# A PEER layer on one core: 8 more tokens by gathered expert rows, 376 dense columns, gate products on GpSimd

## The reference, cut to what matters

```python
def peer(a, w_q, k1, k2, u_exp, v_exp):        # a: (1, 512, 2048)
    ...                                         # two key scores of 128, their best 16 x 16 pairs, the best 16 of these
    experts = jnp.take_along_axis(cand_idx, sel, axis=-1)      # (1, 512, 8, 16), numbers below 16384
    gates = jax.nn.softmax(top, axis=-1)
    def one(args):
        a_c, e_c, g_c = args
        u_sel = jnp.take(u_exp, e_c, axis=0)
        h = jnp.einsum('bthkd,btd->bthk', u_sel, a_c, preferred_element_type=jnp.float32)
        w = (g_c * jax.nn.gelu(h)).astype(a_c.dtype)
        v_sel = jnp.take(v_exp, e_c, axis=0)
        return jnp.einsum('bthk,bthkd->btd', w, v_sel)
```

## Time and profile before

| | us |
|---|---|
| median of 3 runs | 3154.93 (3150.54 to 3158.9) |
| the profiled execution | 3154.94 |
| its span, first to last instruction | 3152.8 |
| TensorE busy | 3112.9 |
| VectorE busy | 2191.3 |
| GpSimd busy | 1066.6 |
| ScalarE busy | 1064.2 |

### The profile page before, as it was taken

The page is one execution under the profiler, slowest core; times in us unless marked ns, Lnnn a source line. Parts: engine busy times, 40 slices in busy tenths (PEclk is TensorE's granted clock), DMA queues, the critical chain, the costliest instruction groups (busy, mean ns, idle before and its releaser), DMA issues.

```text
span 3152.8 us, 42300 instructions
## 1 busy us (share of the span) xinstructions
PE 3112.9 (99%) x16812; PEld 2925.5 (93%) x16812; DVE 2191.3 (70%) x3012; ACT 1064.2 (34%) x1291; POOL 1066.6 (34%) x559
## 2 busy tenths in 40 slices
PE   8999999999999999999999999999999999999998
PEld 6888668899999999999999999999999999999887
DVE  5465653478787777777777647888878887776545
ACT  5234442332333333333333333333333333334422
POOL 1010000028888878788888201101111111110000
PEclk9999999999999999999999999999999999999999
DMA  8472212235455699999999767888888887884322
GB/s 303 144 257 91 94 54 104 96 121 133 115 130 122 176 350 349 322 342 335 352 338 347 276 247 291 309 317 313 302 311 308 315 320 292 319 313 175 107 93 94
DMA packets 190974, 739.10 MB, mean 234 GB/s; under 512 B 69904, under 2 KB 123152, under 8 KB 130944
## 3 DMA queue, kind: packets, MB, share of 16 engines
q1 hardware_dynamic: 90768, 409.55, 35.8%
q0 software_dynamic: 81648, 302.68, 28.3%
q10 hardware_dynamic: 18432, 25.17, 2.3%
HBM read 682.60 MB, written 54.72 MB: 234 GB/s over the span
## 4 chain that ended last, share of the span: by engine, by line
PE 86%; POOL 8%; issue 2%; DVE 2%; DMA 2%; ACT 0%; SPq 0%; DVEq 0%; ACTq 0%; POOLq 0%
PE ps L1492 28%; PE ps L1493 28%; PE ps L1494 28%; POOL gates L460 7%; POOL rows L474 2%; DMA gates<-gates_r,idx_d 1%; PE ps L1665 1%; PE ps L1684 1%; PE ps L1664 0%; DMA raw<-s_v 0%; PE ps L1727 0%; DVE wL L845 0%; DVE ssum L857 0%; DMA rows<-uv_rows,idx_s 0%; PE ps L1674 0%
## 5 line engine op out<-in xcount | busy, mean ns | idle before, releaser
L1492 PE MATMUL ps<-aH,wH 128*128 128x384 f32 (+2 forms) x3088 | 1087.0, 352 | 6.2 <-DVE wL L845 4.0
L1493 PE MATMUL ps<-aL,wH 128*128 128x384 f32 (+2 forms) x3088 | 1083.4, 351 | 0.0
L1494 PE MATMUL ps<-aH,wL 128*128 128x384 f32 (+2 forms) x3088 | 1083.3, 351 | 0.0
L492 ACT ACTIVATE wH<-raw 128x2048 fp32r<-128x2048 f32 x333 | 637.9, 1916 | 893.6 <-PE ps L1494 715.9
L460 POOL DMA_INDIRECT gates<-gates_r,idx_d x384 | 793.2, 2066 | 384.5 <-DVE gates_r L1237 238.3
L845 DVE TENSOR_TENSOR wL<-raw,wH 128x2048 fp32r<-128x2048 f32 x333 | 762.2, 2289 | 230.0 <-ACT wH L492 223.4
L1492 PE MATMUL ps<-actH,wH 128*128 128x384 f32 x2048 | 684.1, 334 | 0.0
L1494 PE MATMUL ps<-actH,wL 128*128 128x384 f32 x2048 | 684.0, 334 | 0.0
L1493 PE MATMUL ps<-actL,wH 128*128 128x384 f32 x2048 | 684.0, 334 | 0.0
L1492 PEld LDWEIGHTS ps<-aH,wH 128*128 128x128 f32 x3088 | 580.7, 188 | 46.7 <-DVE wL L845 5.5
L1494 PEld LDWEIGHTS ps<-aH,wL 128*128 128x128 f32 x3088 | 580.7, 188 | 38.4
(11 more groups left out here) (240 smaller groups left out, 1808.4 us busy)
## 6 DMA issues: line engine op xcount, KB each, us to landing
raw<-s_pu SPq DMA_DIRECT2D x128, 1024.0 KB
raw<-s_pv SPq DMA_DIRECT2D x128, 1024.0 KB
gates<-zeros POOLq DMA_DIRECT2D x24, 1024.0 KB, 8.7
pre<-ut ACTq DMA_DIRECT2D x128, 192.0 KB
pre_in<-pre SPq DMA_DIRECT2D x128, 192.0 KB, 4.4
gate_in<-gates SPq DMA_DIRECT2D x128, 192.0 KB
raw<-s_out SPq DMA_DIRECT2D x16, 1024.0 KB
raw<-s_pq SPq DMA_DIRECT2D x16, 1024.0 KB
```

The costliest lines, as they stand in the source:

```text
L492: A(wH[parity][:, :], raw[parity][:, :], ACT.Copy).then_inc(hi_ready, 1)
L1492: mm(out, wh, xh, start=start, stop=False)
L1493: mm(out, wh, xl, start=False, stop=False)
L1494: return mm(out, wl, xh, start=False, stop=stop)
```

## The change

The dense part shrinks to 376 tokens (`TD`, `TA` = 384 is where the gathered 128 begin), so the matmuls of stages u and v, the stored activations, the gate table and the elementwise passes on them have 376 columns instead of 384. Tokens 376 to 383 are computed by gathered rows in a different layout: 128 partitions hold 16 sets of these 8 tokens, one set for each head and half of its 16 picks, so that 8 more gathers (`B_PICKS`) cover all their 1,024 picks. 32 small transfers bring their expert numbers and gates to these partitions; the 8 token columns are normed, repeated 16 times and transposed to banks 0 to 3 (`spread_tokens`); at the end 16 matmuls with `sel`, in which each token's column picks its 16 partitions, sum the sets. The tiles of v move to banks 4 to 7. The products of activations and gates move from VectorE to GpSimd. 60 picks instead of 64 are worked at up to slot 117, 4 more (`LATE`) in slots 120 to 127, and 72 instead of 64 in stage v.

```diff
 TOPK = 16
 KEYS = 128
 EPS = 1e-6
-TD = 384
-NTD = TD // P
-PICKS = HEADS * TOPK
+BT = 8
+TA = T - P
+TD = TA - BT
+NTD = NT - 1
+SETS = P // BT
+PARTS = SETS // HEADS
+A_PICKS = HEADS * TOPK
+B_PICKS = TOPK // PARTS
+PICKS = A_PICKS + B_PICKS
 GROUP = 8
 NGROUPS = KEYS // GROUP
-BACK = [0, 1, 6, 7]
+BACK = [0, 1, 2, 3]
 WIDE = 2048 // GROUP
 HEAD_U = 4
 ROUTE_U = HEAD_U * HEADS
 ADDS_FIRST = 176
 FIRST_PICK, LAST_PICK = ROUTE_U + 4, KEYS - GROUP - 2
-U_PICKS = 64
+U_PICKS, LATE = 64, 4
 FIRST_SLOT = 2
+B_PREP = 1
 
 
 def u_step(c):
 
-    return (min(max(c, FIRST_PICK), LAST_PICK) - FIRST_PICK) * 2 * U_PICKS // (LAST_PICK - FIRST_PICK)
+    if c > KEYS - GROUP:
+        return 2 * (U_PICKS - LATE + min((c - KEYS + GROUP + 1) // 2, LATE))
+    return (min(max(c, FIRST_PICK), LAST_PICK) - FIRST_PICK) * 2 * (U_PICKS - LATE) // (LAST_PICK - FIRST_PICK)
 
...
@@ -61,7 +70,7 @@
 
 ROW_AT, ROW_USED, ROW_TURN = [], [], []
 for _j in range(PICKS):
-    _at = _j % 3 if _j < U_PICKS else 3 + _j % 2
+    _at = _j % 3 if _j < U_PICKS - LATE else 2 if _j < U_PICKS else 3 + _j % 2
     ROW_USED.append(max([j for j in range(_j) if ROW_AT[j] == _at], default=-1))
     ROW_TURN.append(1 + ROW_AT.count(_at))
     ROW_AT.append(_at)
...
     a_tok = at("a_tok", [KD, T], F, A0 + 32 * KB)
+    b_rep = a_tok[:, :, 0:P]
+    b_small = a_tok[:, :, P:P + BT]
...
             nu = S0["pu"] - ROUTE_U
-            with sp.Fori(0, (KEYS - GROUP - ROUTE_U) // 2) as i:
+            for c in range(ROUTE_U, ROUTE_U + 8):
+                load(nu + c, stream["pu"][c, :, :], c % 2)
+            sp.wait_ge(routed, HEADS)
+            at_b = TD - (NTD - 1) * P
+            for h in range(HEADS):
+                for r in range(PARTS):
+                    dst = slice((h * PARTS + r) * BT, (h * PARTS + r + 1) * BT)
+                    src = slice(h * TOPK + r * B_PICKS, h * TOPK + (r + 1) * B_PICKS)
+                    sp.dma_start(idx_b[dst, :], idx_e[at_b:P, src]).then_inc(b_loaded, 16)
+                    sp.dma_start(gates_b[dst, :], gates_r[at_b:P, NTD - 1, src]).then_inc(b_loaded, 16)
+            with sp.Fori(4, (KEYS - GROUP - ROUTE_U) // 2) as i:
                 for b in range(2):
                     load(nu + ROUTE_U + 2 * i + b, stream["pu"][ROUTE_U + 2 * i + b, :, :], b)
 
...
@@ -368,6 +398,7 @@
                 if c == KEYS - GROUP:
                     for b in range(2):
                         sp.wait_ge(gates_added[b], 16 * NTD * TOPK * HEADS // 2)
+                    sp.wait_ge(b_loaded, 32 * SETS)
                 load_chunk(c - KEYS + GROUP, c % 2)
 
             def load_values(g, last=False):
...
+                    out=gates_flat, out_offset=bass.IndirectOffsetOnAxis(ap=idx_d[0:m, t, c:c + 1], axis=0),
+                    in_=gates_r[0:m, t, c:c + 1], in_offset=None, compute_op=ALU.add).then_inc(gates_added[h % 2], 16)
 
             added = ADDS_FIRST
             for n in range(added):
                 add_gates(n)
 
             pool.wait_ge(a_tok_ready, 1)
-            for j in range(PICKS):
+
+            def gather(j):
+
                 if j == U_PICKS:
                     pool.wait_ge(tile_done, CUM[S0["pv"] - 1])
+                if j == A_PICKS:
+                    pool.wait_ge(b_loaded, 32 * SETS)
                 if ROW_USED[j] >= 0:
                     pool.wait_ge(pick_done, ROW_USED[j] + 1)
+                ids = idx_s[:, j:j + 1] if j < A_PICKS else idx_b[:, j - A_PICKS:j - A_PICKS + 1]
                 pool.indirect_dma_start(
                     out=rows[ROW_AT[j]][:, :, :].rearrange("p a d -> p (a d)"), out_offset=None, in_=a["uv_rows"],
-                    in_offset=bass.IndirectOffsetOnAxis(ap=idx_s[:, j:j + 1], axis=0)).then_inc(row_landed[ROW_AT[j]], 16)
-                if j >= 2:
+                    in_offset=bass.IndirectOffsetOnAxis(ap=ids, axis=0)).then_inc(row_landed[ROW_AT[j]], 16)
+
+            def apply_gates(c, b):
+
+                pool.wait_ge(pre_loaded[b], (c - b) * 8 + 16)
+                pool.wait_ge(gates_loaded[b], (c - b) * 8 + 16)
+                nc.gpsimd.tensor_tensor(pre_in[b][:, :], pre_in[b][:, :], gate_in[b][:, :], ALU.mult).then_inc(act_gated, 1)
+
+            for j in range(U_PICKS - LATE + 1):
+                gather(j)
+                if j >= 1:
                     for n in range(added, min(added + 4 - j % 2, HEADS * NTD * TOPK)):
                         add_gates(n)
                         added = n + 1
+            assert added == HEADS * NTD * TOPK
+            for c in range(GROUP):
+                apply_gates(c, c % 2)
+                if c % 2 == 0 and U_PICKS - LATE + 1 + c // 2 < U_PICKS:
+                    gather(U_PICKS - LATE + 1 + c // 2)
+            for j in range(U_PICKS, U_PICKS + 2):
+                gather(j)
+            for g in range(NGROUPS - 1):
+                for q in range(GROUP):
+                    apply_gates(GROUP * (g + 1) + q, q % 2)
+                    for o in range(v_step(g, q), v_step(g, q + 1)):
+                        if o % 2 == 1 and o // 2 + 2 < PICKS:
+                            gather(o // 2 + 2)
 
 
         @block.scalar
...
+                for o in range(u_step(c), u_step(c + 1)):
+                    if o % 2 == 0:
+                        weigh_pick(o // 2)
                 weight_hi(c - KEYS + GROUP, c - KEYS + GROUP, 0, pre_in[c % 2])
             nv = S0["pv"]
 
...
+            V.scalar_tensor_tensor(a_tok[:, :, TA:T], hT[:, :, TA:T], rtok[:, NTD:NTD + 1],
                                    gain_row[:, :].rearrange("p (a b) -> p a b", a=KD), ALU.mult, ALU.mult).then_inc(a_tok_ready, 1)
             dve.wait_ge(a_tok_ready, 1)
 
             def dot(j):
 
                 dve.wait_ge(row_landed[ROW_AT[j]], 16 * ROW_TURN[j])
+                if j == A_PICKS:
+                    dve.wait_ge(b_tok_done, 1)
+                if j < A_PICKS:
+                    act_of, d = a_tok[:, :, TA:T], dots[:, j:j + 1]
+                else:
+                    act_of = ps[:, 0:4, :].rearrange("p b (c d) -> p (b c) d", c=4)
+                    d = dots_b[:, j - A_PICKS:j - A_PICKS + 1]
                 r3 = rows[ROW_AT[j]][:, 0, :].rearrange("p (a b) -> p a b", a=KD)
-                V.scalar_tensor_tensor(r3, r3, 1.0, a_tok[:, :, TD:T], ALU.mult, ALU.mult,
-                                       accum_out=dots[:, j:j + 1]).then_inc(dot_done, 1)
+                V.scalar_tensor_tensor(r3, r3, 1.0, act_of, ALU.mult, ALU.mult, accum_out=d).then_inc(dot_done, 1)
 
             def add_row(j):
 
                 dve.wait_ge(pick_weighed, j + 1)
                 if j >= 1:
                     dve.wait_ge(pick_done, j)
-                V.scalar_tensor_tensor(hT[:, :, TD:T], rows[ROW_AT[j]][:, 1, :].rearrange("p (a b) -> p a b", a=KD),
-                                       pick_w[:, j:j + 1], hT[:, :, TD:T], ALU.mult, ALU.add).then_inc(pick_done, 1)
+                v3 = rows[ROW_AT[j]][:, 1, :].rearrange("p (a b) -> p a b", a=KD)
+                if j < A_PICKS:
+                    V.scalar_tensor_tensor(hT[:, :, TA:T], v3, pick_w[:, j:j + 1], hT[:, :, TA:T],
+                                           ALU.mult, ALU.add).then_inc(pick_done, 1)
+                elif j == A_PICKS:
+                    V.tensor_scalar(b_acc, v3, pick_wb[:, 0:1], None, ALU.mult).then_inc(pick_done, 1)
+                else:
+                    V.scalar_tensor_tensor(b_acc, v3, pick_wb[:, j - A_PICKS:j - A_PICKS + 1], b_acc,
+                                           ALU.mult, ALU.add).then_inc(pick_done, 1)
+
+            def spread_tokens():
+
+                st.did(V.tensor_tensor(b_small, hT[:, :, TD:TA],
+                                       gains[:, GAINS["ffn"]:GAINS["ffn"] + KD].unsqueeze(2).to_broadcast([P, KD, BT]), ALU.mult))
+                V.tensor_reduce(sel[:, :], ident[:, :].rearrange("p (r t) -> p t r", t=BT), AX, ALU.add).then_inc(sel_ready, 1)
+                st.settle()
+                st.did(V.tensor_tensor(b_small, b_small, rstd[:, TD:TA].unsqueeze(1).to_broadcast([P, KD, BT]), ALU.mult))
+                st.settle()
+                V.tensor_copy(b_rep.rearrange("p k (r t) -> p k r t", t=BT),
+                              b_small.unsqueeze(2).to_broadcast([P, KD, SETS, BT])).then_inc(rep_ready, 1)
 
             def pick_step(o):
 
...
-            def apply_gates(c, b):
-                dve.wait_ge(pre_loaded[b], (c - b) * 8 + 16)
-                dve.wait_ge(gates_loaded[b], (c - b) * 8 + 16)
-                V.tensor_tensor(pre_in[b][:, :], pre_in[b][:, :], gate_in[b][:, :], ALU.mult).then_inc(act_gated, 1)
-
             def weight_lo(c, j, b, src):
                 dve.wait_ge(act_whi, c + 1)
                 V.tensor_tensor(actL[b][:, j, :], src[:, :], actH[b][:, j, :].bitcast(F), ALU.subtract).then_inc(act_wlo, 1)
@@ -1335,7 +1428,7 @@
             def accumulate(k, tiles):
                 dve.wait_ge(tile_done, tiles)
                 h = hT[:, k, 0:TD]
```

(27 more changed lines are left out.)

62 lines of the change are left out of this document (40 added, 22 removed).

## The result

The changed kernel takes **3171.83 us** (median of 5 runs, 3169.16 to 3172.55) against 3154.93 before (5 runs, 3150.54 to 3158.9): ratio **1.0051, 95% interval 1.0037 to 1.0065**. It is slower, by about 17 us; the forecast was 3115.0, with a range of 3107 to 3131. The profiled execution has a span of 3170.8 us, 18.0 over that of before.

What follows compares the result with a forecast made beforehand. The prediction took TensorE's matmul pace, 13.3 ns plus 0.4167 ns a column, to bound the kernel. Its terms, -41.0 + 3.9 - 4.8 + 2.0 = -39.9 us, took 3154.94 to 3115.0 us, range 3107 to 3131.

Steps and rivals of the forecast that it cites:

- Columns: 12,288 matmuls of stages u and v go from 384 to 376 columns, 3.33 ns less each: -41.0 us.
- SP at slot 40: 32 small transfers on SP (13.8 us) delay weight chunk 40, last moment 1128.6: 0 us likely, up to 2.
- Old delay at 1483: u stage: TensorE lost 4.8 us to a late low half behind GpSimd's gate additions; this goes, -4.8 us.
- Turn at slot 120: Slot 120: late gathers delay weight chunk 121 and the next picks; 2 us for the whole turn, upper end 10.
- New TensorE work: 16 transposes in v, 1.7 us, and 16 matmuls of 8 columns in the last group, 2.2: +3.9 us.
- GpSimd's product: 128 gate products on GpSimd in v, 0.8 us each (0.4 to 1.6), hidden if they do not stop VectorE.
- VectorE in v: VectorE's busy time in a v slot goes from 6.68 to 6.44 of 8.16 us, at no cost.
- Rival (c): Slower: GpSimd's product in v stops VectorE, which then sets the pace; at 2.2 us a slot, 3173 us; chance 0.06.
- Rival (d): Columns bring less: if TensorE's weight loads set the pace, nothing is saved, 3156 us; sign 173 ns; chance 0.05.

Runs made afterwards that it cites:

- e2_cols376: The kernel before with 376 columns in all 12,288 matmuls of stages u and v, nothing else changed: 3163.82 us against 3152.31, ratio 1.0036.
- the sweep: The kernel before with only matmul widths changed, 376 and 352 in u, eight widths from 380 to 336 in v; 376 ran at 173.3 ns in u.
- e8_cols368: The kernel before with 368 columns in all matmuls of stages u and v, all else as it was: 3124.62 us against 3153.54, ratio 0.9913.

## Why the prediction was wrong, step by step

- **Columns: forecast -41.0 us, measured 0 in u and -6.9 in v.** This is the step that failed: 34 of the 57 us by which the forecast missed, and without it the changed kernel would have been faster. The words were "Both steps of 128 columns cost 53.3 ns, so the pace is 13.3 ns plus 0.4167 ns a column." The three widths behind that line, 256, 384 and 512, are all multiples of 128, and the line is true for them; it was used at 376, where the changed kernel, e2_cols376 and the sweep have 173.3 ns in u, 3.3 more than the line: just what the 8 columns were to bring. (In v it is 172.2, by the rows of 1504 bytes.)
- **SP at slot 40: forecast 0 to 2 us, measured 7.3 and 1.7 at half clock.** The mechanism was named, its size was not. The 32 transfers took 0.67 us each, where the 0.43 came from two issues of another shape: 21.5 us instead of 13.8. The first stall had also moved the request of chunk 39 from 1104.5 to 1115.3. Even without that, chunk 40 asked for at some 1126 and 8 us later landed is behind the last moment, 1128.6, by an estimated 5.5 us.
- **First gather: no term, measured 8.0 us and 1.5 at half clock.** I took the earlier trace rows as the time of the first dot product and did not ask how much room the 176 additions ahead of its gather had. They had almost none, and the time they need moves with the width of the matmuls beside them: by the fourth head, 11 us more with 376 columns than with 384.
- **Old delay at 1483: forecast -4.8, gone.** By the distances of matmuls it was 4.7 us. Right: no wait over 0.5 us between 1150 and 1850.
- **Turn at slot 120: forecast +2, measured 3.0** (1.5 us each at 1857.8 and 1876.0). Right in mechanism and within its range.
- **New TensorE work: forecast +3.9, measured 6.8.** The transposes took 1.7 us, as forecast. The small matmuls are 32 instructions, not 16, at 112 ns, 3.6 us, and behind them ten matmuls ran at half clock, 1.5 us:

```profile
2891.00:2896.00 5.00, 5.00 (x43) 5.00 (x41) 1.88 (x2) 1.91 (x1) 0.00 (x0) 1.00 0.26 104
2896.00:2901.00 5.00, 5.00 (x22) 5.00 (x22) 3.60 (x6) 2.38 (x4) 0.00 (x0) 0.66 0.61 202
```

- **GpSimd's product: forecast 0.8 us, measured 1.00** undisturbed and 1.24 in the mean (L521). **VectorE in v: forecast 6.44 us a slot, measured 6.8** of 8.27 (660.2 us busy from 2000 to 2800), the rest being passes lengthened by products. Both stayed hidden, as forecast: TensorE waits 1.1 us in the whole v stage. Rival (c) did not come.
- **Rival (d)**, that the columns bring nothing, was right on this term (its time was 3156) and had a chance of 0.05, on the ground that the 120.0 ns at 256 columns exclude another pace-setter. They exclude weight loads as the cause, and say nothing about 376. The sign that the prediction had set for it, a distance of 173 ns, is what u shows.

The measured terms give -6.9 + 6.8 - 4.7 + 9.5 + 9.0 + 3.0, and about 1.5 for single waits in v: 18.2 us, where the spans differ by 18.0. The chances fail in the same place: 0.95 of them shared the column term, so the range was one opinion about slack and none about the pace.

## What to carry to other kernels

A pace read at 256, 384 and 512 columns says nothing about 376: time the very width in the kernel's own stream before counting on it, and try a few columns more as well, since a wider matmul can be the cheaper one. A queue that feeds the first use of a new stage (here the additions ahead of the first gather) has to be given a slack in the sum, not only the stage's mean load: with narrower matmuls beside it, it was 12 us later here, with the same list of work. Small transfers on the queue that loads weights belong one pair at a time between the loads.

## What the runs showed of the hardware

- The distance between fp32r matmuls with 128 x 128 weights is not monotone in the width: 378 columns 173.2 ns, 380 171.2, 382 173.3; 352 161.1, 356 160.1. With 376 columns it also depends on how the operand's rows lie: 173.3 ns at rows of 1536 and 2048 bytes, 172.2 at 1504.
- A gate addition by GpSimd takes 1.54 us with VectorE idle (14 in a row in e8_cols368), and 2.0 us in the mean over the 176 of the head stage, up to 5.2. Three heads of them take 331 us beside matmuls of 384 columns, 342 beside 376, 343 beside 380 and 354.5 beside 368.
- A VectorE pass with both inputs in SBUF and a GpSimd product that meet lengthen one another: dot product 2.94 instead of 2.28 us, product 2.19 instead of 1.00. With one input in PSUM the pass stays at 0.53 to 0.55 us.
- Small transfers from SBUF to SBUF cost SP 0.67 us each to issue, where its loads of expert products and gates took 0.33 and 0.43 in the median.
- 32 matmuls of 8 columns at 112 ns each were followed by ten matmuls at half clock (1.2 GHz), with TensorE busy without a gap ahead of them.
